# Two blocks of a diffusion-style transformer on one core: the start addresses of the SBUF tensors moved by 128 and by 160 bytes

## The reference, cut to what matters

```python
def mlp(s, shift, scale_m):
    hm = rms_norm(s, g_norm2) * (1.0 + scale_m) + shift
    return jnp.square(jax.nn.relu(hm @ w_mlp1)) @ w_mlp2

x_new = x_new + gt2 * mlp(x_new, sh2, sc2)            # block 1: 1024 -> 4096 -> 1024
x = x + gm * sq_relu_mlp(modulate(rms_norm_2(x, g_mlp[l]), sm, cm), w_mlp1[l], w_mlp2[l])
ctx = ctx + gm_c * sq_relu_mlp(modulate(...), w_mlp1[l], w_mlp2[l])   # block 2, first layer only
```

## Time and profile before

| | |
|---|---|
| median of three runs | 2681.04 us (2679.49 to 2682.08) |
| profiled execution, first to last instruction (span) | 2676.4 us |
| what lies around that span, as median less span | 4.6 us |
| TensorE busy with matmuls | 2521.2 us, 94% of the span |
| VectorE, ScalarE, GpSimd busy | 1557.1, 931.9, 115.6 us |
| DMA engines busy (mean of 16) | 15.4% by the loads from SyncE's queue, 9.1% by GpSimd's |

### The profile page before, as it was taken

How to read it: one execution, slowest core, us unless ns; L and a number is a source line. 1 busy time by engine, 2 the same in 40 slices (tenths; PEclk the granted TensorE clock), 3 DMA queues, 4 the chain that set the end, 5 groups by cost and what they waited for, 6 DMA issues and landing times.

```text
span 2676.4 us, 45804 instructions
## 1 busy us (share of the span) xinstructions
PE 2521.2 (94%) x19622; PEld 2039.4 (76%) x19622; DVE 1557.1 (58%) x2412; ACT 931.9 (35%) x1599; POOL 115.6 (4%) x222
## 2 busy tenths in 40 slices
PE   6999988779999999999998999999999998999997
PEld 3777667667887788877777888888887776788886
DVE  3355577767656788854675556545445466534444
ACT  3344443223235223342553432222233254422322
POOL 0000001120100010000000000000000000000000
PEclk8999899989999999999999999999999999999999
DMA  6000000004653555411002123333321102222210
GB/s 277 32 32 1 33 3 4 5 5 172 221 214 118 181 189 190 172 44 59 5 32 79 64 95 126 126 126 126 126 95 44 63 32 86 93 97 103 95 63 32
DMA packets 32202, 244.88 MB, mean 91 GB/s; under 512 B 3616, under 2 KB 3776, under 8 KB 20992
## 3 DMA queue, kind: packets, MB, share of 16 engines
q1 hardware_dynamic: 11808, 164.83, 15.4%
q0 software_dynamic: 20192, 77.11, 9.1%
HBM read 239.83 MB, written 2.10 MB: 90 GB/s over the span
## 4 chain that ended last, share of the span: by engine, by line
PE 85%; DVE 9%; issue 3%; ACT 2%; DMA 1%; POOL 0%; DVEq 0%; SPq 0%; ACTq 0%
PE ps L337 57%; PE ps L2190 2%; PE ps L2419 2%; PE ps L949 1%; PE ps L2447 1%; PE ps L1370 1%; PE ps L2463 1%; PE ps L905 1%; PE ps L367 1%; PE ps L2465 1%; PE ps L2464 1%; PE ps L368 1%; PE ps L369 1%; PE ps L950 1%; PE ps L951 1%
## 5 line engine op out<-in xcount | busy, mean ns | idle before, releaser
L337 PE MATMUL ps<-hh,ws 128*128 128x512 f32 x3216 | 752.9, 393 | 10.9 <-DVE hh L524 7.1
L337 PEld LDWEIGHTS ps<-hh,ws 128*128 128x128 f32 x3216 | 601.3, 188 | 144.9 <-issue 15.6
L318 ACT ACTIVATE ws<-raw 128x1024 fp32r<-128x1024 f32 x295 | 308.6, 1049 | 430.0 <-PE ps L337 396.6
L326 DVE TENSOR_TENSOR ws<-raw,ws 128x1024 fp32r<-128x1024 f32 x295 | 359.8, 1221 | 151.5 <-ACT ws L318 151.4
L337 PE MATMUL ps<-g,ws 128*128 128x512 f32 x1536 | 364.4, 396 | 0.0
L337 PEld LDWEIGHTS ps<-g,ws 128*128 128x128 f32 x1536 | 286.4, 188 | 66.6
L337 PE MATMUL ps<-gg,ws 128*128 128x512 f32 x960 | 227.6, 398 | 2.1 <-ACT ws L318 2.1
L1807 DVE SCALAR_TENSOR_TENSOR xT<-ps,mods,xT 128x512 f32<-128x512 f32 x120 | 90.0, 750 | 227.8 <-PE ps L337 220.5
L337 PEld LDWEIGHTS ps<-gg,ws 128*128 128x128 f32 x960 | 181.3, 189 | 46.4 <-ACT ws L318 2.5
L1970 DVE TENSOR_TENSOR sq<-sq 128x512 f32<-128x512 f32 (+1 forms) x128 | 80.0, 625 | 142.4 <-ACT sq L1947 142.4
L1947 ACT ACTIVATE sq<-ps 128x512 f32<-128x512 f32 (+1 forms) x128 | 69.4, 542 | 258.7 <-PE ps L337 244.6
(11 more groups left out here) (378 smaller groups left out, 3571.1 us busy)
## 6 DMA issues: line engine op xcount, KB each, us to landing
raw<-in_w_m SPq DMA_DIRECT2D x32, 2048.0 KB, 7.8
raw<-in_w_ada POOLq DMA_DIRECT2D x80, 512.0 KB, 3.9
raw<-in_w_mlp SPq DMA_DIRECT2D x16, 2048.0 KB, 8.0
ar<-in_w_ada POOLq DMA_DIRECT2D x48, 512.0 KB, 3.9
raw<-in_w_in SPq DMA_DIRECT2D x8, 2048.0 KB, 7.4
raw<-in_w_mg SPq DMA_DIRECT2D x8, 1536.0 KB, 7.3
raw<-in_w_out SPq DMA_DIRECT2D x6, 2048.0 KB, 8.1
raw<-in_w SPq DMA_DIRECT2D x5, 2048.0 KB, 7.5
```

What stands on the lines that cost most here:

```text
L318: e.activation(w_of(n)[0], pieces[n][2], ACT.Copy).then_inc(*hi(n))
L326: e.tensor_tensor(l, pieces[n][2], h.bitcast(F32), ALU.subtract).then_inc(*lo(n))
L337: m = e.matmul(o, a, b, start=n == 0, stop=n == 3 * kt - 1)
```

## The change

A tensor of 32 float32 columns (128 bytes a partition) is placed ahead of all others, and `mi` grows from 8 to 16 columns (32 to 64 bytes). Nothing else is changed; nothing reads or writes the added bytes. The order of the instructions and what they wait for is the same on all five engines; line numbers grow by one.

```diff
@@ -120,6 +120,7 @@
         def sb(name, shape, dt=F32, stack=ctx):
             return stack.enter_context(nc.sbuf_tensor(name, shape, dt))
 
+        sb("spare", [P, 32])
         raw = sb("raw", [P, RAWN, 4096])
         ws = sb("ws", [P, WSN, 2, 1024], F32R)
         hh = sb("hh", [P, 2, KT, T], F32R)
@@ -132,7 +133,7 @@
         ones = sb("ones", [P, P])
         rs = sb("rs", [P, T])
         sq = sb("sq", [P, 2, T])
-        mi = sb("mi", [P, 8])
+        mi = sb("mi", [P, 16])
         REST = 18432
```

## The result

The changed kernel takes 2667.77 us (median of four runs, 2665.64 to 2668.68) against 2681.56 (median of four, 2679.49 to 2684.59): ratio 0.9947, interval 0.9933 to 0.9961. It is faster by 13.8 us, where 29.0 were forecast. The measured time lies at the very top of the stated range; the gain is less than half of the forecast.

What follows compares the result with a forecast made beforehand. TensorE, busy 2521.2 of 2676.4 us, was taken to bound the kernel through its matmul rate. Gains of 17.5 + 8.7 + 1.3 + 0.5 + 1.0 = 29.0 us gave 2647.4, plus 4.6 gave 2652.0 us; range 2640 to 2668.

Steps and rivals of the forecast that it cites:

- The first step: MLPs and merge: the end is set by the rate at which matmuls follow one another, so rate changes count in full.
- fetched in pieces of 64 bytes: float32r operands: a 2048-byte run starting mid-piece touches 33 pieces instead of 32, costing 6.5 ns; chance 0.84.
- A: 512 moving columns out of the arena (`g`, `gg`, `yy`): 2688 matmuls, 6.5 ns less each, 17.5 us gained.
- B: 256 moving columns from the arena, line 337 (`hc`, `gc`): 1776 matmuls, 4.9 ns each, 8.7 us gained, ends 0 and 12.8.
- C: 256 columns in groups interleaved with other work (lines 367 to 369, 2464 and twins): 408 matmuls, 1.3 us gained, ends 0 and 4.
- D (line 2190): Stationary operand out of the arena on line 2190: 96 matmuls, 5.4 ns less each, 0.5 us gained.
- E: Tiles of `hh` right behind `hc`, up to 42: half their 0.05 us excess goes, 1.0 us gained, ends 0 and 2.1.
- around the span: The runs' median lies 4.6 us above the profiled span of 2676.4, untouched by the change and added to the forecast.
- Costed at nothing: float32 matmuls (lines 480, 559), VectorE, ScalarE and loads: assumed not to change, 0 us.
- No change: the place: Rival: the arena is slow for its place in upper SBUF, not its start; 2681 us, chance 0.10.
- More: 256 counts as well: Rival: multiples of 256 bring another 6.5 ns on `hh` and the 2688 matmuls, 38 us more, 2614; chance 0.03.
- Slower: one residue for all: Rival: all tensors congruent modulo 256 make TensorE's reads meet writes of `ws`; 2696.6 us at 10 ns each, chance 0.03.

Runs made afterwards that it cites:

- experiment 4: Changed kernel with `hh` alone moved to 32 bytes past a multiple of 64, `raw` and `ws` 128 bytes lower: 2698.02 against 2676.94 us before, ratio 1.0079.
- experiment 5: Changed kernel with 160 instead of 128 bytes in front, every tensor 32 bytes higher: 2667.67 against 2679.05 us before, ratio 0.9956.
- experiment 6: Changed kernel with the 128 bytes placed behind `ws` instead of in front of `raw`: 2696.87 against 2679.05 us before, ratio 1.0068.
- Experiment 3: Changed kernel with `hc2` and `gc2` alone moved 32 bytes on: 2658.80 against 2676.94 us before, ratio 0.9935.
- experiment 1: Kernel before with only `mi` grown from 8 to 16 columns, moving the arena 32 bytes: 2666.11 against 2676.94 us, ratio 0.9962.
- experiment 8: Changed kernel with `hc2` and `gc2` alone 16 bytes behind their places: 2662.02 against 2680.60 us before, ratio 0.9933; changed kernel beside it 2667.30.
- Experiment 2: Changed kernel with `mi` back at 8 columns, so only the 128 bytes in front: 2678.40 against 2676.94 us before, ratio 1.0004.
- experiment 7: Changed kernel, second block's activations shifted (four kernels) or 256 bytes between `ws` and `hh` (fourth listed); single runs: 2670.58, 2674.16, 2672.64, 2665.92, 2679.07 us.

## Which steps of the prediction held, and which failed

The first step, that the MLPs and the merge go at the matmuls' rate and a change of rate counts in full, holds: TensorE's busy time fell by 14.6 us and the time by 13.8.

**The reading "fetched in pieces of 64 bytes" failed.** It was the inference on which the whole sum was built. Experiments 4, 5 and 6 refute it: a start at a multiple of 256 was slow (44.80 us for `gg`), starts 32 past a multiple of 64 were fast (43.52). What the runs show in its place is D: the 512-column products reached 226.7 ns where their two operands began at the same byte modulo 256 (and in one case 16 bytes apart), and nowhere else. The evidence was in the trace, in the earlier trace rows: the cost was the same whether the odd tensor was moving or stationary. I took that for a property of the tensor; it is as well one of the pair, and the slower rival, with its residues modulo 256, had the right quantity with the wrong sign.

**A, forecast 17.5 us, measured 16.6 to 17.0.** By the rows: ten groups of 192 (six of `gg` and `yy`, four of `g` in the last layer) by 1.28 us, and 32 tiles of `g` in the first layer by 5.60 - 5.47 = 0.13, 17.0. Counted from each of the 2688 matmuls' starts to the next instruction's start, 631.2 us became 614.7. Right in size, but by luck, for the wrong reason: moving the arena to a multiple of 64 happened to make it congruent to `ws`.

**B, forecast 8.7 us of gain, measured 2.3 us of loss.** This is the step that failed in the sum: "half of the aligned 512-column price". A tile has 2.87 instead of 2.84 us, some 0.03 by 74 tiles. It makes 11 of the 15.2 us by which the gain fell short. I had set the bound at "118.3, no gain", and left out a loss; the trace of before had no row for 256 columns at D = 0, and nothing excluded one. Experiment 3 shows that this term is the start's doing: 32 bytes bring the tile to 2.80 us and the kernel to 2658.8, where experiment 1, at the rates of the changed kernel, took 2666.1 beside it. By the tiles, 64 in the MLP by 0.07, it would be 4.5 us of these 7.3.

**C, forecast 1.3, measured a loss of some 0.3.** The same width; from start to start the `hc` matmuls of lines 2463 to 2465 take 0.1 us longer in all, those of lines 949 to 951 0.1, those of lines 367 to 369, which also wait, 0.07.

**D (line 2190), forecast 0.5, measured 0.5.** 8 groups of 12, by 0.07 us each.

**E, forecast 1.0, measured 0.8.** The tile of `hh` behind `hc` has 5.47 instead of 5.49, 0.8 us over 42 tiles. A tile of `g` behind `gc` now has the same 0.03 over its 5.44, which the sum of A above holds already. So the excess comes with the change of width, and its size with D of the context's tile, not with a start modulo 64. In the traces a 512-column tile behind a 256-column one needs some matmuls until it runs at its own rate: before the change the first nine intervals of `hh` behind `hc` last 224 to 236 ns, after it the first five 229 to 235, in experiment 8 the first two 231 to 233; from there on each has 226.7.

These add up to -16.6 + 2.3 + 0.3 - 0.5 - 0.8 = -15.3 us; measured are -13.8 by the medians (-10.5 to -18.0 by the interval of the ratio) and -11.1 by the two profiled spans. The order of the instructions is the same, so the 4.2 us between can be looked for by the starts of the same rows before and after. The merge's first tile of `gg` starts at 640.58 and 642.32 us: 1.7 us are lost ahead of it. From line 480's two matmuls at 2040.01 (2031.77 after) to the first group of line 2190, 30.12 us became 31.97. From there to the 144 matmuls of `hh` ahead of the last MLP's first `g`, 246.14 became 246.60. Experiment 2, in which every operand's D is as before, has 641.64, 31.74 and 247.18 at these places. So most of this is not the change's: it differs from execution to execution, and the profiled one of before was a fast one.

For the second place the clock shows how. TensorE waits 2.8 us there for the context's norm. The windows of before and after, the columns as in the earlier trace rows:

```profile
2035.00:2060.00 25.00, 19.90 (x81) 15.68 (x80) 17.97 (x33) 12.96 (x23) 1.47 (x6) 0.86 0.09 31
```

```profile
2027.00:2052.00 25.00, 19.81 (x73) 15.09 (x72) 18.21 (x33) 13.01 (x23) 1.47 (x6) 0.80 0.09 31
```

The clock was granted at 0.80 instead of 0.86 in these 25 us, and TensorE did 73 matmuls instead of 81: the stretch at the lower of its two levels (1.2 instead of 2.4 GHz) lasted 10.2 us instead of 6.8. Experiment 2 has 0.80 there as well.

**The rest of the sum around the span.** The 4.6 us "around the span" were too much: the changed kernel's profiled run took 2667.05 us for a span of 2665.3, 1.8 us. By the same 1.8 the profiled execution of before took 2678.2 us, less than any of its timed runs. It cost the forecast nothing, since span and 4.6 together are the median, but a gain read from the two profiled spans alone comes out 2.8 us short.

**Costed at nothing, and rightly:** float32 matmuls. The two lines of the earlier trace rows after:

```profile
L481 PE MATMUL ps<-sq,ones x12: 591/592/592, 807.2 to 2649.3; 128*128 128x512 f32 x12
...
L560 PE MATMUL ps<-ar,cst x22: 589/591/668, 80.3 to 2112.8; 128*128 128x512 f32 x22
```

**The rivals.** "No change: the place" is refuted by the result and by experiment 4. So is what hung on 16-byte lines (the Trainium skill, SBUF — State Buffer, section "🔬 SBUF: two separate sides"), as a forecast for this change; that a start 32 bytes past a multiple of 64 costs nothing in itself, which also follows from it, agrees with experiment 5. "More: 256 counts as well" is refuted by experiments 1 and 2 as far as a start goes. "Slower: one residue for all" is refuted: one residue for all is what makes the kernel fast.

One more rival has to be ruled out. `raw` and `ws` are congruent modulo 256 in every kernel here, and ScalarE, VectorE and the loads work on both while TensorE multiplies; the slow matmuls could be waiting for one of these. The trace of before says no. Of the 191 intervals between the starts of the last layer's first 192 matmuls with `g`, 49 fall where VectorE, ScalarE, GpSimd and all DMA engines are idle. They last 233.4 ns in the mean, and the 12 during which VectorE, ScalarE and a DMA are all at work last 233.3.

## What to carry to other kernels

When two groups of the same instruction differ in rate, list everything in which they differ, relations between the operands included, and move one tensor at a time before naming a cause; a run in which the supposed cause is present in an unchanged tensor, as `gg` in experiment 4, is worth more than one that merely confirms. In a kernel bound by float32r matmuls of these shapes, try starts for the weights buffer and the 512-column activations that agree modulo 256 bytes, and other offsets for the 256-column ones: here the first is worth 0.5%, and both together 0.7%. A price for a shape that the trace doesn't hold at the new setting needs a bound on both sides of zero.

## What the runs showed of the hardware that I had not expected

The period of back-to-back float32r matmuls with a 128x128 stationary operand depends on the difference of the two operands' start addresses modulo 256 bytes, by up to 3% at 512 columns (226.7 to 233.4 ns) and in another order at 256 columns (116.7 to 119.9 ns), and not on either start alone. What ran just before counts as well (E above, and experiment 6 beside 4). When the stationary operand was the displaced one, it cost as much: line 2190 has a D of 32 in the earlier trace rows and of 224 in experiment 3, and 12 matmuls took 2.79 us in both. The row of experiment 3:

```profile
1220.80 2.96 PE L2191 MATMUL ps<-ws,hc 128*128 128x512 f32 x12
1223.60 5.62 PE L2191 MATMUL ps<-ws,hh 128*128 128x512 f32 x24
```

(2.80 us here, by the rounding of the starts.) Why the difference matters wasn't shown. In the trace of before, the weight load recorded with each matmul of the first MLP starts 2 to 4 ns after it and takes 187 or 188 ns, with `hh` as with `gg`, so the two operands are read side by side at either rate; a conflict of the two read streams in SBUF would fit, but no run measured it. Two things stay open. The period isn't a function of D alone: at 256 columns 16 bytes gave 2.80 us a tile beside a `g2` with the same offset, and 2.85 beside one with none, and at 512 columns experiments 4 and 6 differ at the same two addresses. And with the stationary operand 16 bytes on (D of 240, line 2190 in experiment 8) nothing was lost, while with the moving one 16 bytes on (D of 16, `g2` in experiment 7) each matmul took 5 ns more; whether the sign or the role decides, no run tells apart:

```profile
1211.93 2.88 PE L2200 MATMUL ps<-ws,hc 128*128 128x512 f32 x12
1214.65 5.60 PE L2200 MATMUL ps<-ws,hh 128*128 128x512 f32 x24
```

12 matmuls of experiment 8 in 2.72 us, as in the changed kernel.
